# A decoder step on one core: the set-up of the attention heads with norm sums in columns, latents returned feature-major, decode two places sooner

## The reference

```python
cq, ckv, kr, gq, gk, gv, gr, gg = jnp.split(x @ w_in, idx, axis=-1)   # 384, 256, 64, ... columns
q = (rms_norm(cq, q_norm) @ w_uq).reshape(B, T, MLA_HEADS, MLA_NOPE + MLA_ROPE)
q_rope = apply_rope(q_rope, cos, sin); k_rope = apply_rope(kr, cos, sin)
ckv = rms_norm(ckv, kv_norm)              # returned as new_ckv, k_rope as new_krope
s = (q_lat . ckv + q_rope . k_rope) * MLA_SCALE      # causal, then
p = softmax(s); o = p @ ckv
# GLA of the sample: S = exp(g) S + k v ; o = q S ; rms_norm(o) * silu(gg)
```

## Time and profile before

| | us |
|---|---|
| median of 3 runs | 1493.43 (1492.27 to 1493.61) |
| the profiled execution | 1484.69 |
| its span | 1483.0 |
| mean granted TensorE clock | 0.958 of full speed |
| PE busy | 1384.6 (93%) |
| DVE busy | 615.8 (42%) |
| ACT busy | 414.1 (28%) |
| POOL busy | 169.6 (11%) |

### The profile page before, as it was taken

The page is one execution under the profiler, slowest core; times in us unless marked ns, Lnnn a source line. Parts: engine busy times, 40 slices in busy tenths (PEclk is TensorE's granted clock), DMA queues, the critical chain, the costliest instruction groups (busy, mean ns, idle before and its releaser), DMA issues.

```text
span 1483.0 us, 22328 instructions
## 1 busy us (share of the span) xinstructions
PE 1384.6 (93%) x8873; PEld 1275.7 (86%) x8873; DVE 615.8 (42%) x960; ACT 414.1 (28%) x680; POOL 169.6 (11%) x199
## 2 busy tenths in 40 slices
PE   7998989999568999799999999999999999999996
PEld 7986868887346776589999999999999999999996
DVE  4122223443575665556553231333314223232558
ACT  4122232233423333454351220302203022130235
POOL 4324432000030000013200000000000000003022
PEclk9999999998769998699999999999999999999998
DMA  6658887312210001131120020201202011030103
GB/s 239 234 183 254 287 286 215 86 30 105 69 36 18 10 1 57 43 101 63 39 86 29 29 86 0 85 28 49 64 0 86 27 57 57 3 110 0 57 1 115
DMA packets 101858, 123.16 MB, mean 83 GB/s; under 512 B 11739, under 2 KB 86645, under 8 KB 101654
## 3 DMA queue, kind: packets, MB, share of 16 engines
q1 hardware_dynamic: 95638, 105.36, 22.4%
q0 software_dynamic: 6144, 16.79, 3.6%
HBM read 108.19 MB, written 13.93 MB: 82 GB/s over the span
## 4 chain that ended last, share of the span: by engine, by line
PE 64%; DVE 6%; ACT 4%; issue 1%; POOL 0%; DVEq 0%; ACTq 0%; POOLq 0%
PE psum L2079 23%; PE psum L2107 21%; PE psum L1802 6%; PE psum L1326 6%; PE psum L2046 2%; PE psum L1633 2%; PE psum L1642 1%; DVE pT_lo L1712 1%; ACT p_rows L1672 1%; DVE softmax_stats L1694 1%; ACT pT_hi L1678 1%; PE psum L1384 0%; ACT z_T L1884 0%; PE psum L2040 0%; ACT z_T L2333 0%
## 5 line engine op out<-in xcount | busy, mean ns | idle before, releaser
L2136 ACT ACTIVATE hid_tmp<-psum 128x1032 f32<-128x1032 f32 x32 | 33.1, 1034 | 531.5 <-PE psum L2079 527.7
L351 PE MATMUL psum<-xTh,win_hi 128*128 128x344 f32 (+1 forms) x432 | 150.7, 349 | 9.6 <-DVE xTl L404 9.6
L2079 PE MATMUL psum<-x_hi,w_hi 128*128 128x344 f32 x720 | 153.3, 321 | 0.0
L2079 PE MATMUL psum<-x_lo,w_hi 128*128 128x344 f32 x720 | 152.8, 320 | 0.0
L2079 PE MATMUL psum<-x_hi,w_lo 128*128 128x344 f32 x720 | 152.0, 319 | 0.0
L2107 PE MATMUL psum<-hid_hi,w_hi 128*128 128x344 f32 x672 | 142.5, 320 | 0.0
L2107 PE MATMUL psum<-hid_lo,w_hi 128*128 128x344 f32 x672 | 142.3, 320 | 0.0
L351 PE MATMUL psum<-xTl,win_hi 128*128 128x344 f32 (+1 forms) x432 | 141.8, 328 | 0.0
L2107 PE MATMUL psum<-hid_hi,w_lo 128*128 128x344 f32 x672 | 141.8, 319 | 0.0
L351 PE MATMUL psum<-xTh,win_lo 128*128 128x344 f32 (+1 forms) x432 | 141.7, 328 | 0.0
L2201 DVE TENSOR_TENSOR z_T<-z_T,psum 128x1032 f32<-128x1032 f32 x48 | 59.0, 1229 | 186.5 <-PE psum L2107 186.5
(11 more groups left out here) (379 smaller groups left out, 2265.7 us busy)
## 6 DMA issues: line engine op xcount, KB each, us to landing
mlp_raw<-in_w SPq DMA_DIRECT2D x64, 512.0 KB, 4.2
k_pages<-in_pages SPq DMA_DIRECT2D x128, 160.0 KB, 3.1
v_pages<-in_pages POOLq DMA_DIRECT2D x128, 128.0 KB, 4.8
win_raw<-in_w_in SPq DMA_DIRECT2D x17, 512.0 KB, 7.0
scratch<-proj_stage SPq DMA_DIRECT2D x13, 516.0 KB, 5.9
x_T_raw<-in_x_T SPq DMA_DIRECT2D x6, 688.0 KB, 9.2
z_T<-in_x_T SPq DMA_DIRECT2D x3, 1376.0 KB, 6.3
out_y_T<-z_T SPq DMA_DIRECT2D x12, 344.0 KB, 2.4
```

What stands on the lines that cost most here:

```text
L351: mm = pe.matmul(psum[0:M, 3 * (m % 2) + b, 0:BLK], w[:, m % 2, k, 0:M], x[:, k, b * BLK:(b + 1) * BLK], start=(k == 0 and i == 0), stop=( ...
L2079: mm = pe.matmul(psum[:, 3 * (i % 2) + b, 0:BLK], w[:, i % 2, k], x[:, k, C3[b]], start=(k == 0 and n == 0), stop=(k == KD - 1 and n == 2))
L2136: act.activation(ht[:, i % 2, :].rearrange("p (b c) -> p b c", b=3), mlp_set(i), ACT.Relu).then_inc(h_free, 1)
```

## The change

**Decode.** Scores begin at place 13 in place of 15, so the last value product comes at place 40 and not in the GLA slots; the samples' q steps come at places 11 and 12, and w_uq and w_uk for them are loaded behind the third weight tile, to another address. The gates move by a place.

**GLA of the sample.** `sO` takes the 128 x 32 query block as weights and the 128 x 128 state as moving operand (16 matmuls as before, in four column groups), so outputs come as rows of 128 values. Their squares are summed by ACT, `ss` goes, and four transposes (`gTs`) bring them back.

**MLA set-up.** Squares are added on DVE first, and a matmul whose weights are 128 x 128 of the summed squares and whose moving operand is one column of ones gives the sums of 128 tokens as a column (`pe_norm_sums`, 8 matmuls, slot 47 `nk` for ckv, later `nq` for cq). Root and two Newton steps run on 128 x 8. For ckv the column is spread over partitions by 8 matmuls with the identity (`bc`). cq isn't scaled by its norm at all: the norm weight goes into the split, and 1/rms times the softmax's scale goes into exp's scale and the row maximum's factor, one per query row. The rope part of the key is loaded twice and swapped by transfers in place of 12 matmuls. Latents are stored feature-major, with no transposes; the host transposes them. All lo parts are on DVE, none on POOL. Only the 1,024 prompt columns are handled, in two blocks of 512 in place of three of 344. Products of q's rope part come before the GLA's last transposes.

```diff
-        SCORE_AT = {15 + 7 * u // 4: u for u in range(NU)}
-        VALUE_AT = {p + 1: u for p, u in SCORE_AT.items() if u < NU - 1}
-        GATE_AT, GATE_LN_AT = {22: 0, 25: 1, 27: 2, 29: 3, 32: 4}, 35
+        SCORE_AT = {13 + 7 * u // 4: u for u in range(NU)}
+        VALUE_AT = {p + 1: u for p, u in SCORE_AT.items()}
+        GATE_AT, GATE_LN_AT = {23: 0, 25: 1, 27: 2, 30: 3, 32: 4}, 34
         X_MEAN_AT = {8: 0, 9: 1, 10: 2}
-        SSQ_AT, QN_AT, QS_AT, KN_AT, SN_AT, MT_AT, W4_AT, OM_AT, OT_AT, UV_AT = 9, 13, 14, 20, "sn", "mT", "w4", "oM", "oT", "uv"
+        SSQ_AT, QN_AT, QS_AT, KN_AT, SN_AT, MT_AT, W4_AT, OM_AT, OT_AT, UV_AT = 9, 11, 12, 20, "sn", "mT", "w4", "oM", "oT", "uv"
...
+                if m == 0:
+                    sp.dma_start(wuq[:], a["w_uq"][0].rearrange("(k p) c -> p k c", p=P)).then_inc(duq_loaded, 16)
+                    sp.dma_start(wukT[:], a["w_uk_T"].rearrange("p (h r) -> p h r", h=HEADS)).then_inc(duq_loaded, 16)
...
-                    for b in range(NB):
-                        c = (f * NB + b) * 2
-                        mm = pe.matmul(o[:, c:c + 2], state[b // 4][:, b % 4, f, :], qd[:, f, b, :], start=True, stop=True)
-            elif name == "ss":
-                pe.wait_ge(osq_done, 1)
-                mm = pe.matmul(o[:, 0:32], const("ones"), osq[:], start=True, stop=True)
+                    for bq in range(2):
+                        for g in range(4):
+                            mm = pe.matmul(o[32 * g:32 * g + 32, (2 * f + bq) * DV:(2 * f + bq + 1) * DV], qd[:, f, 4 * bq + g, :],
+                                           state[bq][:, g, f, :], start=True, stop=True)
...
+            elif name == "nk":
+                pe.wait_ge(cksq_done, 3)
+                mm = pe_norm_sums(pe, o, cksq[0])
...
+            dve_rstd_rms(dve, 0)
+            dve.sem_inc(rk_done, 1)
+            lo_of(dve, "wr"), lo_of(dve, "cq0")
+            for s in range(SLOTS + 3, SLOTS + 6):
+                dve_slot(dve, s)
+            lo_of(dve, "cq1"), lo_of(dve, "cq2")
+            gated(dve, 2), gated(dve, 3), gated(dve, 4)
             variance(dve, 1)
-            gated(dve, 3), gated(dve, 4)
+            dve_ckv_scaled(dve, 0), dve_ckv_scaled(dve, 1)
...
+        def pe_norm_sums(pe, o, squares):
+
+            for t in range(8):
+                mm = pe.matmul(o[:, t:t + 1], squares[:, t * P:(t + 1) * P], const("ones")[:, 0:1], start=True, stop=True)
+            return mm
...
+        def pe_rope_in(pe, pr):
+            for b in range(2):
+                mb.begin(pe, ("qr", pr, b))
+                mb.full(passes(pe, mb.of(("qr", pr, b)), [((wrh[:, pr, k], wrl[:, pr, k]), (cqh[:, k, C2[b]], cql[:, k, C2[b]])) for k in range(3)]))
+
+        def pe_rope_swap(pe, pr):
+            for b in range(2):
+                mb.begin(pe, ("qs", pr, b))
+                pe.wait_ge(qx_done, 2 * pr + b + 1)
+                mb.full(pe.matmul(mb.of(("qs", pr, b)), const("swap"), xr[:, pr, C2[b]], start=True, stop=True))
...
+            pe.wait_ge(rk_done, 1)
+            for b in range(2):
+                mb.begin(pe, ("bc", b))
+                for j in range(4):
+                    t = 4 * b + j
+                    mm = pe.matmul(mb.of(("bc", b))[:, j * P:(j + 1) * P], rstdc[:, 0, t:t + 1].broadcast_to([P, P]), ident, start=True, stop=True)
+                mb.full(mm)
             split(pe, "cq2")
-            for pr in range(2):
-                for b in range(3):
-                    mb.begin(pe, ("qr", pr, b))
-                    c = slice(b * BLK, (b + 1) * BLK)
-                    mb.full(passes(pe, mb.of(("qr", pr, b))[:, 0:BLK],
-                                   [((wrh[:, pr, k], wrl[:, pr, k]), (cqh[:, k, c], cql[:, k, c])) for k in range(3)]))
-                for b in range(3):
-                    mb.begin(pe, ("qs", pr, b))
-                    pe.wait_ge(qx_done, 3 * pr + b + 1)
-                    mb.full(pe.matmul(mb.of(("qs", pr, b))[:, 0:BLK], const("swap"), xr[:, pr, b * BLK:(b + 1) * BLK], start=True, stop=True))
-            pe.wait_ge(rows_stored, 64)
+            pe_rope_in(pe, 0)
+            for t in range(NORM_A, 8):
+                pe_gla_task(pe, ("gT", t))
+            pe_gla_task(pe, ("gTs",))
+            pe_rope_swap(pe, 0)
+            pe_rope_in(pe, 1)
+            mb.begin(pe, ("nq",))
+            pe.wait_ge(cqsum_done, 2)
+            mb.full(pe_norm_sums(pe, mb.of(("nq",)), cqsq[:, 0]))
+            pe_rope_swap(pe, 1)
...
-            NORMS = (("ck", "sqc", ckraw, 2, KVN), ("cq", "sqq", cqraw, 3, QN))
-            for j, (name, nm, raw, nk, g) in enumerate(NORMS):
-                for b in range(3):
-                    mb.wait(dve, (nm, b))
-                    mb.free(dve.tensor_scalar(var[:, j, b * BLK:(b + 1) * BLK], mb.of((nm, b))[:, 0:BLK], 1.0 / (nk * P), EPS,
-                                              ALU.mult, ALU.add), (nm, b))
-                mb.read(dve, (nm, 2))
-                dve.sem_inc(mv_done, 1)
-            lo_of(dve, "wr")
...
-            for j, (name, nm, raw, nk, g) in enumerate(NORMS):
-                dve.wait_ge(mr_done, j + 1)
-                newton(dve, rst[:, j], var[:, j], ntmp[:])
-                for k in range(nk):
-                    dve.scalar_tensor_tensor(raw[:, k], raw[:, k], cols[:, g + k:g + k + 1], rst[:, j], ALU.mult, ALU.mult).then_inc(my_done, 1)
-            for name in ("cq0", "cq1", "cq2"):
-                lo_of(dve, name)
-            dve.wait_ge(gst_stored, 80)
-            for t in range(TT):
-                c0, n = tok(t)
-                mb.wait(dve, ("tok", t))
-                mb.free(dve.tensor_copy(tout[0:n, t, :], mb.of(("tok", t))[0:n, 0:KVR + ROPE]), ("tok", t))
...
+            dve_krope(dve)
+            lo_of(dve, "ck0"), lo_of(dve, "ck1")
+            dve.wait_ge(cqsq_done, 3)
+            for k in (1, 2):
+                ins = dve.tensor_tensor(cqsq[:, 0], cqsq[:, 0], cqsq[:, k], ALU.add)
+                ins.then_inc(cqsum_done, 1)
+                dve.wait_ge(cqsum_done, k)
+            lo_of(dve, "kr"), lo_of(dve, "uv")
+            dve_rope(dve, 0)
+            lo_of(dve, "q0")
+            dve_var_rms(dve, 1, mb, ("nq",), 3 * P)
+            dve_rope(dve, 1)
+            lo_of(dve, "q1")
+            dve_rstd_rms(dve, 1)
+            dve.tensor_scalar(rqs[:], rstdc[:, 1, :], SCALE, None, ALU.mult)
+            dve.tensor_scalar(nrqs[:], rstdc[:, 1, :], -SCALE, None, ALU.mult).then_inc(rq_done, 1)
+            dve.wait_ge(rq_done, 1)
...
-                                   scale=SCALE, bias=stat[:, v % 4, 1:2], accum_out=stat[:, v % 4, 2:3]).then_inc(ex_done, 1)
+                                   scale=rqs[:, v % 8:v % 8 + 1], bias=stat[:, v % 4, 1:2], accum_out=stat[:, v % 4, 2:3]).then_inc(ex_done, 1)
...
-                    dve.tensor_scalar(stat[:, v % 4, 1:2], stat[:, v % 4, 0:1], -SCALE, None, ALU.mult).then_inc(nb_done, 1)
+                    dve.tensor_scalar(stat[:, v % 4, 1:2], stat[:, v % 4, 0:1], nrqs[:, i:i + 1], None, ALU.mult).then_inc(nb_done, 1)
...
-    y_T=(D, T), ckv_prompt=(1, 1, TP, KVR), krope_prompt=(1, 1, TP, ROPE),
-    gla_prompt=(1, 1, HEADS, DK, DV), ckv_sample=(1, NB, 1, KVR), krope_sample=(1, NB, 1, ROPE),
-    gla_sample=(1, NB, HEADS, DK, DV))
+    y_T=(D, T), ckv_T=(KVR, TP), krope_T=(ROPE, TP), gla_prompt=(1, 1, HEADS, DK, DV),
+    ckv_sT=(KVR, NB), krope_sT=(ROPE, NB), gla_sample=(1, NB, HEADS, DK, DV))
```

More of the change, by code:

```diff
@@ L501, in pe_decode @@
             if p in VALUE_AT:
-                pe_values(pe, VALUE_AT[p])
+                u = VALUE_AT[p]
+                key = ("val", u)
+                dq.begin(pe, key)
+                pe.wait_ge(pet_done, u + 1)
+                pe.wait_ge(vp_loaded[u % 2], 16 * PG * (u // 2 + 1))
+                for j in range(PG):
+                    g = j % 4
+                    mm = pe.matmul(dq.of(key)[32 * g:32 * g + 32, 0:KVR], pet[:, u % 2, j, :], vpages[:, u % 2, j, :],
+                                   start=(j < 4), stop=(j >= PG - 4))
+                dq.full(mm)
             if p in SCORE_AT:
@@ L591, in act_decode @@
             if p in VALUE_AT:
-                act_values(act, VALUE_AT[p])
+                key = ("val", VALUE_AT[p])
+                dq.wait(act, key)
+                dq.free(act.activation(o_all[:, unit(VALUE_AT[p])[2], :], dq.of(key)[:, 0:KVR], ACT.Copy), key)
             if p in SCORE_AT:
@@ L1050, in act_gla @@
                 act_slot(act, s)
+            act.wait_ge(wr_loaded, WR_BASE + 64)
+            hi_of(act, "wr")
+            act.wait_ge(cq_loaded, 16)
+            for k in range(3):
+                hi_of(act, f"cq{k}")
             act_squares(act, 7)
@@ new lines, in dve_var_rms, with dve_rstd_rms, dve_ckv_scaled @@
+        def dve_var_rms(dve, i, bank, key, n):
+            bank.wait(dve, key)
+            bank.free(dve.tensor_scalar(rvar[:, i, :], bank.of(key)[:, 0:8], 1.0 / n, EPS, ALU.mult, ALU.add), key)
+            bank.read(dve, key)
```

(16 more changed lines are left out.)

454 lines of the change are left out of this document (206 added, 248 removed).

## The result

| | us |
|---|---|
| before, median of 4 runs | 1492.85 (1489.81 to 1493.61) |
| after, median of 4 runs | 1452.69 (1450.04 to 1464.59) |
| ratio | 0.9767, 95% interval 0.9736 to 0.9798 |
| the profiled executions | 1484.69 before, 1451.67 after (spans 1483.0 and 1450.0) |

The change is faster by 2.3%, some 35 us by the ratio (34.8 = 0.0233 x 1493) and 40 by the medians. 1461.0 was predicted, with a range of 1449 to 1475. The two profiled executions lie 33.0 us apart; the sum of the prediction was 32.4.

The account below looks back on a forecast made before the run. The prediction took the set-up between GLA and head units as a chain on DVE that PE follows. Slots, set-up, decode and head units: -3.8 - 29.6 + 0 + 1 = -32.4, from 1493.43 to 1461.0 us; range 1449 to 1475.

Parts of the forecast that it names:

- Slots, -3.8: GLA slots up to the last state update: sO saves 3.5 us, clock behind slot 44 2.5, nk costs 2.2.
- New chain, 55.8 us: Set-up from last state update to first head product: nine items, mostly DVE work, sum 55.8 us before low-clock losses.
- items 2 to 9: Set-up: gT 4, bc, scalings; ckv norm; gT 5 to 7; nine large operations; two rope pairs; small Newton, scales; v.
- Item 4: Set-up: gT 5 to 7 between PE and DVE 3.5 us, gTs and two small ones 1.2: 4.7 us.
- Item 9: Set-up: v's 48 matmuls, 11.3 us of PE, 5.2 remaining uncovered, then ACT's and DVE's head parts: 6.8 us.
- The low clock, +4 on top: Set-up: half clock on PE costs 2.5 us at v's start and 1.5 through q's first rope products.
- Decode, 0: Decode: work and pace stay, PE still waits 8.8 us for key pages; 0, near term -4 to +4 us.
- Head units, +1: Head units: exp's second column operand in 32 units costs 1 us, bounds 0 and +10.9; the maximum's factor no dearer.
- half-clock set-up: Rival: PE stays at 0.50 clock through q's second products and all of v; gain 19.4 us, 1474; chance 0.13.
- Key waits go: Rival in the decode: the earlier start also removes the waits for key pages, -8.8 us more, 1452; chance 0.10.
- ACT's line: Rival in the set-up: DVE's cut is paid back waiting for ACT, 1 us at each of 14 steps; 1475 to 1479; 0.08.
- Slower: Rival in the decode: SP's line starves it, keys come later for every unit, 1502 us; chance 0.02.

Follow-up runs that it names:

- pool_busy: Changed kernel with two additions of 128 x 1,024 put on GpSimd in the set-up, needed by nothing before the head units: 1455.92 us.
- gaps_filled: Changed kernel with head 0's parts made ahead of v's and DVE's krope and v-weight lo parts moved into its two waits for ACT: 1448.29 us, ratio 0.9734.
- again2: The changed kernel run once more, unedited, as a comparison on the same chip: 1456.26 us, ratio 0.9768.
- decode_mid: Changed kernel with the decode's score and value products one place later, scores from place 14: 1450.81 us, ratio 0.9731.
- b_ck_lo_dve: Kernel before, with ckv's lo parts on DVE in place of GpSimd, ahead of cq's: 1483.19 us, ratio 0.9955.

## Why the prediction was right, step by step

- **The mechanism**: right. The set-up was a chain on DVE, and the gain is there: -35.2 us, with -32.9 in all. What shows it is the chain itself, priced step by step ahead and met step by step (below), and two edits of the changed kernel: 3.4 us that DVE is held in pool_busy are 3.4 us of the stage, and 2.3 us of DVE's work taken from ahead of the second swap in gaps_filled bring the swap and v 2.3 us sooner. The edits of the kernel before take only 4.2, 1.6 to 2.1 and 1.0 to 1.5 us out of the stage; no run takes the norm in rows back into the changed kernel, so most of the 35 us is not split between the parts of the change by an experiment.
- **Slots, -3.8**: measured -4.3. sO's price of 2.1 was too high, 1.08 measured, the lower bound; nk's +2.2 too high as well, 1.95 for the 16 instructions, or 1.55 after the 0.4 of `ss`. By the Trainium skill, "TensorE: Matmul & The Clock Gate", section "LDWEIGHTS (loading the stationary operand)", the estimate was 1.7 us: 0.122 us each here lies between the page's 0.107 and the row's 0.14. The clock behind slot 44 was full in the first trace, as said, but fell there in again2 and decode_mid; the 2.5 us counted for it is the uncertain term. Slot 44's own products gave 4.3 us on average (5.4 to 1.08) and nk took 1.5, which leaves 1.5 for the clock and the rest of the stage.
- **New chain, 55.8 us**: in the trace of after, gT 4 starts 8.6 us behind the state's end (9.0 was said) and `bc` 9.1 (9.7), and items 2 to 9 end 14.5, 18.2, 20.9, 31.5, 37.8, 45.5, 47.1 and 53.7 us behind it. Predicted were 14.1, 18.0, 22.7, 33.8, 40.2, 47.1, 49.0 and 55.8. Item 4 was 2.0 us too dear (2.7 for 4.7: gT 5 to 7 hardly wait between PE and DVE); every other item is within 0.8. Item 9 is right by luck: its 5.2 us doesn't follow from its own terms, 11.3 less 8.3 is 3.0. In the trace v's products begin later and run on for 4.5 us behind item 8, then come ACT's and DVE's parts of the last tile, 1.3, which the item left out, and the head's lo part, 0.8: 6.7 for 6.8.
- **The low clock, +4 on top**: the step that was mis-sized. q's first rope products and v's ran at 1.00 in the first two traces. The second swap took a loss of 1.5 us (3.37 for the 1.88 of the first swap), which is in item 7, and the head's first 12 products 1.9 (4.62 for 12 x 0.23), which are behind the mark. In again2 it did come, mostly elsewhere: behind the state update PE is at 0.50, `bc` starts 2.4 us later than in after, v's products take 1.0 us longer, and the set-up is 56.8 us. Four of the six traces with this stage unedited are of this kind (55.7 to 56.8 us), so the low clock is worth 2 to 3 us in these and 1.9 on average, in place of 4. Windows of 5 us (length; busy time of PE, PEld, DVE, ACT, POOL; granted clock; DMA share; GB/s), after first, then again2:

```profile
365.00:370.00 5.00, 2.06 (x16) 1.29 (x14) 5.00 (x6) 2.50 (x9) 0.00 (x0) 1.00 0.85 242
```

```profile
365.00:370.00 5.00, 4.95 (x22) 2.89 (x21) 4.39 (x10) 2.47 (x3) 0.00 (x0) 0.50 1.11 301
```

  So the set-up went from 90.8 to 55.6 us where 89.4 to 59.8 was said: -35.2 for -29.6.
- **Decode, 0**: wrong by 4 us, at the end of its near term (-4 to +4). The key waits stayed, as argued; what wasn't priced is the GLA's first load of v, 1.3 us more, beside 1.9 of key waits. What delays that load was not shown; decode_mid's 1.3 us fits the places, b_ck_lo_dve's 2.7 doesn't.
- **Head units, +1**: measured +2.2, with a scatter of 3 us between executions. The exp's second operand costs 0.088 us, 32 x 0.088 = 2.8 of ACT, and PE's waits for pT_lo grew by 3.2 (16.2 on average to 19.4). At 0.15 us a unit for the exp and DVE's factor together that is an estimate of 21 units of 32, where the prediction had the exp lead "in a few units only". By the Trainium skill, "ScalarE: Activation LUTs", section "What ACT_TABLE_LOAD costs", it is 93 ns, and the estimate from it, 3.0 us, was nearer than the value taken from rows. DVE's factor was said to be "no dearer" by such rows; it is by 0.06, 2 us in 32.
- **8.7 us between profile and median, carried over**: right as arithmetic, but its cause wasn't asked. The clock goes with it: 0.958 in that one execution, 0.952 in executions of 1491 us. For the changed kernel the profile was nearer to its own median (1451.67 for 1453.6 over the 14 unedited runs). That is why 1461.0 lies 7 to 8 us above the median though the sum of the stages is right to 1 us: -4.3, -35.2, +4.0, +2.2 and +0.4 for -3.8, -29.6, 0, +1 and 0. That the sum comes out so close is luck: two errors of 4 to 6 us, the decode and the set-up, cancel.
- **The rivals**: half-clock set-up, no: 0.87 of full speed there in the first trace, and 0.76 to 0.80 in the four slower ones, where v's products lost 1.0 us at most. Key waits go: no, 9.1 us after for 8.8. ACT's line: it does hold DVE twice, 1.18 and 1.13 us, not at each of 14 steps. Slower, and "doesn't do what it says": no.
- **What would show it**: no DVE instruction over 1.3 us but the norm of 128 x 1,536 (1.76), which was there before and which the sentence should have excepted; no POOL in the set-up, slot 44 below 2.2 us with full clock behind it, three key waits: all seen. The first head product came at 415.5 and not near 424.

## What to carry to other kernels

Cut the trace of several executions at the same marks before a number is read off one of them: here a single stage moved by 3 to 6 us between executions, mostly with the clock, as much as most terms of the sum. Per-token factors belong in a column or in an operand that is there anyway, not in rows of 1,024; the operand has a price too, here some 3 us in 32 exps. Where two engines share a chain, look at what is held by work on a third: taking two lo parts off GpSimd and giving them to the engine that set the pace was a gain.
